# Sparse attention in three passes, an earlier second projection unit, forgetting values by channels, forgetting queries on 128 partitions, and narrower block levels in a two-model kernel

## The reference

```python
# sparse attention: 16 heads of 128 in 4 groups; 4 key blocks of 64 all chosen at this length
s = q @ k.T * scale; p = softmax(where(valid, s, NEG))
o = g0 * (p_c @ v_cmp) + g1 * (p_s @ v_sel) + g2 * (p_w @ v_win)
y = (silu(gate) * o) @ w_out

# mixer of the second model (w_in gives gq, gk, gv, gz, gb, ga, fq, fk, fv, ff)
a_mat = where(strict, (k @ k.T) * decay * beta, 0)         # gated delta heads, 4 of 128
u, w = triangular_solve(a_mat + eye, [v * beta, k * beta * exp(gc)])
s = fq @ fk.T * 64**-0.5 + (c_i - c_j); o_fox = softmax(causal(s)) @ fv   # 8 heads of 64
h = h + concat(o_gdn, o_fox) @ w_out
h = h + swiglu(rmsnorm(h)); return rmsnorm(h)[16:]
```

## Time and profile before

| | |
|---|---|
| median of 3 runs | 990.27 us (990.2 to 990.33) |
| profiled execution: its time | 988.4 us |
| its span | 986.6 us |
| granted TensorE clock, mean | 0.998 |
| PE busy | 968.6 us, 98% |
| PE weight loads | 853.3 us, 86% |
| DVE busy | 621.9 us, 63% |
| ACT busy | 472.1 us, 48% |
| POOL busy | 116.4 us, 12% |

### The profile page before, as it was taken

The page is one execution under the profiler, slowest core; times in us unless marked ns, Lnnn a source line. Parts: engine busy times, 40 slices in busy tenths (PEclk is TensorE's granted clock), DMA queues, the critical chain, the costliest instruction groups (busy, mean ns, idle before and its releaser), DMA issues.

```text
span 986.6 us, 15771 instructions
## 1 busy us (share of the span) xinstructions
PE 968.6 (98%) x6364; PEld 853.3 (86%) x6364; DVE 621.9 (63%) x887; ACT 472.1 (48%) x816; POOL 116.4 (12%) x117
## 2 busy tenths in 40 slices
PE   8999999999999999999999999999999999999996
PEld 7988778778998999998778789987888899999885
DVE  4964457556884655666654477986655666766533
ACT  6234446446545543455544456664435454444432
POOL 1000022010410000101320003212320101111000
PEclk9999999999999999999999999999999999999999
DMA  8745445445556753332015454522001355555551
GB/s 310 265 155 173 164 136 174 170 168 187 186 181 213 261 209 129 126 131 87 1 38 177 170 180 151 176 93 86 8 37 44 129 192 191 194 194 191 196 188 43
DMA packets 23372, 150.55 MB, mean 153 GB/s; under 512 B 3548, under 2 KB 3832, under 8 KB 5896
## 3 DMA queue, kind: packets, MB, share of 16 engines
q1 hardware_dynamic: 22960, 149.39, 43.4%
q10 hardware_dynamic: 344, 0.18, 0.1%
HBM read 148.50 MB, written 1.05 MB: 152 GB/s over the span
## 4 chain that ended last, share of the span: by engine, by line
PE 95%; DVE 2%; DMA 1%; ACT 1%; issue 0%; POOL 0%; POOLq 0%; SPq 0%; DVEq 0%; ACTq 0%
PE psum L689 91%; PE psum L768 1%; PE psum L1083 1%; DMA ring<-in_weights 1%; PE psum L1390 0%; DMA h<-in_x 0%; DVE ring_parts L1901 0%; ACT R L1509 0%; PE psum L1089 0%; PE psum L1251 0%; PE psum L1212 0%; PE psum L1255 0%; DVE xT_parts L529 0%; DVE xn L2437 0%; ACT L520 0%
## 5 line engine op out<-in xcount | busy, mean ns | idle before, releaser
L1901 DVE TENSOR_TENSOR ring_parts<-ring,high_parts 128x1024 fp32r<-128x1024 f32 (+1 forms) x272 | 334.0, 1266 | 161.1 <-ACT high_parts L1502 160.2
L1502 ACT CAST high_parts<-ring 128x1024 fp32r<-128x1024 f32 x268 | 268.0, 1049 | 204.9 <-PE psum L689 164.0
L689 PE MATMUL psum<-xT_parts,high_parts 128*128 128x256 f32 (+1 forms) x960 | 216.9, 285 | 2.8 <-DVE ring_parts L1901 2.3
L689 PE MATMUL psum<-xT_parts,ring_parts 128*128 128x256 f32 (+1 forms) x672 | 192.4, 286 | 0.0
L689 PE MATMUL psum<-high_parts,R_parts 128*128 128x512 f32 (+1 forms) x592 | 177.5, 375 | 1.1 <-DVE R_parts L529 1.1
L689 PE MATMUL psum<-high_parts,xT_parts 128*128 128x512 f32 (+1 forms) x528 | 171.0, 400 | 0.0
L689 PEld LDWEIGHTS psum<-xT_parts,high_parts 128*128 128x128 f32 x960 | 162.8, 189 | 4.4 <-DVE ring_parts L1901 2.9
L689 PE MATMUL psum<-R_parts,high_parts 128*128 128x256 f32 x832 | 156.5, 277 | 0.0
L689 PEld LDWEIGHTS psum<-R_parts,high_parts 128*128 128x128 f32 x832 | 130.3, 188 | 0.0
L689 PEld LDWEIGHTS psum<-xT_parts,ring_parts 128*128 128x128 f32 x672 | 126.7, 189 | 0.1
L689 PEld LDWEIGHTS psum<-high_parts,R_parts 128*128 128x128 f32 (+1 forms) x592 | 105.0, 179 | 21.8 <-issue 1.3
(11 more groups left out here) (306 smaller groups left out, 1085.0 us busy)
## 6 DMA issues: line engine op xcount, KB each, us to landing
ring<-in_weights SPq DMA_DIRECT2D x136, 1024.0 KB, 4.9
h<-in_x SPq DMA_DIRECT2D x4, 256.0 KB, 4.4
ring<-in_weights SPq DMA_DIRECT2D x4, 256.0 KB, 5.7
G<-in_gains SPq DMA_DIRECT2D x2, 512.0 KB, 7.3
out<-xn SPq DMA_DIRECT2D x2, 512.0 KB, 3.1
R<-in_ret_tabs SPq DMA_DIRECT2D x1, 768.0 KB, 11.4
tab<-in_tabs SPq DMA_DIRECT2D x1, 663.5 KB, 6.0
G<-in_p_t SPq DMA_DIRECT2D x1, 512.0 KB, 6.9
```

The costliest lines, as they stand in the source:

```text
L689: return pe.matmul(out, lhsT, rhs, start=first, stop=last, skip_group_check=True)
L1502: act.copy(as_r(hi), value).then_inc(sem("units_high"), 1)
L1901: return dve.tensor_tensor(as_r(value), value, value_of(hi), ALU.subtract)
```

## The change

- Start: unit 1 is loaded in halves, unit 3 ahead of the retention tables, and split_up_to(3) stands where split_up_to(2) did; ACT makes a small copy before its first real work, and PE a matmul without use among the turns.
- ret_w_out's units are ordered by row half first, then by column half; yT 1 is turned behind row half 0 of column half 0.
- Sparse attention's P·V becomes three one-pass products: V is split once into four high and four low parts, the turned probabilities of each step by ACT (high) and DVE (low). nsa_order puts step i+1's T ahead of step i's O.
- Forgetting queries: each head has its own 128x256 area with zeros in the other head's 64 rows, cleared by POOL; the meta columns are left out; DVE writes two halves. fox_scores then uses all 128 partitions.
- Forgetting values are made by channels (fv, 4 tiles, from A units) and turned on PE (vT) behind level 1's z; the order around Q is changed with it.
- Levels: z and y are computed for the odd blocks' columns alone.
- End: the last unit's products go row block by row block, and row block 0 is normed and stored by itself, in halves on three engines.

```diff
-    b("ret_w_out", 0, D, 16)
+    units.extend(("ret_w_out", "B", k0 + 4 * i, c0) for k0 in (0, 8) for c0 in (0, 512) for i in range(2))
...
-    b("w_in_2", 3080, 512)
+    a("w_in_2", 3080, 512)
...
+    order = [("S", 0), ("S", 1), ("N", 0), ("N", 1), ("C", 0), ("G", 0), ("T", 0), ("G", 1), ("S", 2), ("N", 2)]
+    last = len(STEPS) - 1
+    for i in range(last):
+        order += [("T", i + 1)] + [("G", i + 2)] * (i < 2)
+        if i + 3 <= last:
+            order.append(("S", i + 3))
+        order.append(("O", i))
+        if i + 3 <= last:
+            order.append(("N", i + 3))
+    return order + [("O", last)]
...
-             ("fin", 7), ("A", 2), ("A", 0), ("fv", 0, 0)] + [("Lz", 0, c) for c in level_chunks(0)]
-    order += [("fv", 0, 1), ("Q", 1), ("fv", 0, 2), ("Qm", 1), ("Q", 2), ("fv", 1, 0), ("Qm", 2), ("kv", 1), ("fv", 1, 1),
-              ("kv", 2), ("fv", 1, 2), ("Fs", 0), ("kv", 0)]
-    beside = {1: ([("Fn", 0), ("Fs", 1)], [("Ft", 0)]), 2: ([("Fn", 1), ("Fs", 2)], [("Fo", 0), ("Ft", 1)]),
+             ("fin", 7), ("A", 2), ("A", 0), ("fv", 0)] + [("Lz", 0, c) for c in level_chunks(0)]
+    order += [("Q", 1), ("fv", 1), ("Qm", 1), ("Q", 2), ("fv", 2), ("Qm", 2), ("kv", 1), ("fv", 3), ("kv", 2), ("Fs", 0),
+              ("kv", 0)]
+    beside = {1: ([("Fn", 0), ("vT", 1), ("Fs", 1)], [("vT", 2), ("vT", 0), ("Ft", 0)]), 2: ([("Fn", 1), ("Fs", 2)], [("Fo", 0), ("Ft", 1)]),
...
+        def fox_query(hd):
+            return nw[:, hd * T:(hd + 1) * T] if hd < 4 else R[:, R3 + (hd - 4) * T:R3 + (hd - 3) * T]
...
+        def odd_blocks(ap, lv):
+            return ap.rearrange("p (b two m) -> p b two m", two=2, m=LEVELS[lv])[:, :, 1, :]
...
-            for u in (1, 2):
-                unit(u, weights[u])
+            half = UNIT // 2
+            load("second_half", ring[:, UNIT:UNIT + half], weights[1, :, 0:half])
+            sp.dma_start(ring[:, UNIT + half:2 * UNIT], weights[1, :, half:UNIT]).then_inc(sem("unit_in1"), 16)
+            unit(2, weights[2])
+            unit(3, weights[3])
             load("ret_in", R[:, R4:R4 + NRT], ret_tabs)
-            unit(3, weights[3])
...
+                if f == 1:
+                    mm(psum[:, 3, 0:T], xn[:, 0:P], xn[:, 0:T], True, True)
...
-                        v0 = R2 + br * 1024 + k * 512 + g * P
-                        ins = mm(o.rearrange("p (n q) -> p n q", n=nh), R[:, v0:v0 + P], p_t[:, k], False,
-                                 br == 1 and k == kt - 1)
+                        v = [part[:, g * P:(g + 1) * P] for part in nsa_value_parts(2 * br + k)]
+                        p_t = [part[:, :, k * T // kt:(k + 1) * T // kt] for part in turned_p(i, br)]
+                        ins = parts3(mm, o.rearrange("p (f t) -> p f t", f=2), v, p_t, False, br == 1 and k == kt - 1)
...
-                    q0 = R3 + c0 + M + b * P
-                    mm(o, R[p0:p0 + FD, q0:q0 + P], R[p0:p0 + FD, R3 + 4 * TM + c0:R3 + 4 * TM + c0 + n], True, False)
+                    mm(o, fox_query(hd)[:, b * P:(b + 1) * P], R[:, R3 + 4 * TM + c0:R3 + 4 * TM + c0 + n], True, False)
...
+                first = M if name == "fin" and j < 4 else 0
                 for k in range(KD):
-                    ins = parts3(product, bank[:, 0:TM], w(k, slice(j % 2 * P, (j % 2 + 1) * P)), x_src(k, 0, TM),
+                    ins = parts3(product, bank[:, first:TM], w(k, slice(j % 2 * P, (j % 2 + 1) * P)),
+                                 x_src(k, first, TM - first), k == 0, k == KD - 1)
...
+            def value_rows(c):
+                t0, m = CHUNKS[c]
+                wait_read(pe, main, ("fv", 3))
+                bank = aux.open(pe, ("vT", c))
+                for j in range(4):
+                    ins = pe.transpose(bank[0:m, j * P:(j + 1) * P], value_cols(j, c), ident)
+                aux.full(ins, ("vT", c))
...
-                        ins = mm(bank[0:n, hd * n:(hd + 1) * n], of_head(level_rows(lv, c), c, hd), mat(PTb, C_ALL, c, hd),
-                                 True, True)
+                        ins = mm(bank[0:n, hd * n // 2:(hd + 1) * n // 2].rearrange("p (b m) -> p b m", m=LEVELS[lv]),
+                                 of_head(level_rows(lv, c), c, hd), odd_blocks(mat(PTb, C_ALL, c, hd), lv), True, True)
...
-            for c in range(2):
-                for t in range(TT):
+            for t in range(TT):
+                for c in range(2):
                     for k in range(2):
                         ins = parts3(product, banks[c, t], hidden_src(20 + k, t), w(k, slice(c * 512, (c + 1) * 512)),
...
+            act.wait_ge(sem("eps_set"), 1)
+            act.copy(cst[:, 9:10], eps1)
...
-                    bank = wait(aux, ("wT", i))
-                    c0 = i % 2 * 1024 + 512
-                    aux.free(act.copy(PTb[:, c0:c0 + 512], bank), ("wT", i))
+                    for br, name in enumerate(("sT", "wT")):
+                        bank = wait(aux, (name, i)).rearrange("p (f t) -> p f t", f=2)
+                        act.copy(as_r(turned_p(i, br)[0]), bank).then_inc(sem("turned_p"), 1)
...
-            split_up_to(2)
+            split_up_to(3)
...
+                        dve.wait_ge(sem("turned_p"), 2 * i + br + 1)
+                        hi, lo = turned_p(i, br)
+                        aux.free(dve.tensor_tensor(as_r(lo), bank, value_of(hi), ALU.subtract), (name, i))
...
+                    if j < 4:
+                        dve.wait_ge(sem("query_zeros"), 2)
+                        for half in range(2):
+                            rows_ = slice(half * FD, (half + 1) * FD)
+                            ins = dve.scalar_tensor_tensor(fox_query(2 * j + half)[rows_, :], bank[rows_, M:TM],
+                                                           float(FD) ** -0.5, token_scale[rows_, M:TM], ALU.mult, ALU.mult)
...
+                if jj == 4:
+                    pool.memset(nw[:, :], 0.0).then_inc(sem("query_zeros"), 1)
+                if jj == 7:
+                    pool.memset(R[:, R3:R3 + 4 * T], 0.0).then_inc(sem("query_zeros"), 1)
...
-            norm(7)
+            for t in range(TT):
+                total = last_sums(t)
+                pool.wait_ge(sem("last_sums"), 2 * t + 1)
+                own.then_wait(pool.tensor_scalar(total[:, 2:3], total[:, 0:1], EPS, None, ALU.add))
+                pool.wait_ge(sem("last_sums"), 2 * t + 2)
+                root = rstd[:, 14 + t:15 + t]
+                own.then_wait(pool.tensor_tensor(root, total[:, 1:2], total[:, 2:3], ALU.add))
+                pool.tensor_tensor(root, root, power, ALU.pow).then_inc(sem("last_root"), 1)
```

More of the change, by code:

```diff
@@ L231, in main_uses @@
     u += [(("fin", j), "dve") for j in range(8)]
-    u += [(("fv", c), "act") for c in range(3)]
+    u += [(("fv", j), "dve") for j in range(4)]
     u += [(("gz", t), "act") for t in range(TT)]
@@ L236, in main_uses @@
         u += [(("fg", n), "dve"), (("fu", n), "dve")]
-    u += [(("dn", c, t), "dve") for c in range(2) for t in range(TT)]
+    u += [(("dn", c, t), "dve") for t in range(TT) for c in range(2)]
     return u
@@ L289, in splits_beside @@
 def splits_beside(kind, key):
-    return kind in ("fin", "gz") or kind == "fv" and key[1] < 2 or kind == "mo" and key != [1, 1]
+    return kind in ("fin", "fv", "gz") or kind == "mo" and key != [1, 1]
 def mixer_uses():
@@ L918, in _, with retention_output @@
                         turn_half("yT", 0, R3)
[L920 to L927 removed]
+            def retention_output(k0, c):
+                for kk in (k0, k0 + 4):
+                    w, product = next_unit(4)
+                    for t in range(TT):
+                        bank = main.at(("ro", c, t)) if kk else main.open(pe, ("ro", c, t))
+                        for k in range(4):
+                            ins = parts3(product, bank, out_src(kk + k, *rows0[t]), w(k, slice(0, 512)), kk + k == 0,
+                                         kk + k == 15)
+                        if kk == 12:
+                            main.full(ins, ("ro", c, t))
+            for k0 in (0, 8):
+                for c in range(2):
+                    if (k0, c) == (0, 1):
+                        pe.wait_ge(sem("ret_y"), 8)
+                        turn_half("yT", 1, R3)
+                    retention_output(k0, c)
             def ple(n, added, ready):
@@ L1759, in _ @@
                     split_up_to(item + HIGH - 1, 1)
-                if kind == "fv" and key[0]:
-                    c = key[1]
+                if kind == "vT":
+                    c = key[0]
                     m = CHUNKS[c][1]
-                    bank = main.wait(act, ("fv", c))
+                    bank = aux.wait(act, ("vT", c))
                     c0 = R3 + 8 * TM + c * 512
-                    main.free(act.activation(R[0:m, c0:c0 + 512], bank[0:m, :], ACT.Copy,
-                                             scale=rstd[:, 9 + c:10 + c] if c else 1.0), ("fv", c))
+                    aux.free(act.activation(R[0:m, c0:c0 + 512], bank[0:m, :], ACT.Copy,
```

(10 more changed lines are left out.)

152 lines of the change are left out of this document (103 added, 49 removed).

## The result

The changed kernel takes 974.03 us (median of 4 runs, 973.14 to 975.99) against 990.3 in the same job (4 runs, 990.2 to 990.39): ratio 0.9843, 95% interval 0.9832 to 0.9855. The profiled execution took 973.14 us with a span of 971.6, 15.0 under the span before. The page: busy times, and the chain by engine.

A forecast was written before the change was run, and what follows sets the result against it. TensorE, busy 98% of the span, was taken to bound the kernel. Gains and losses summed to -11.05 us, so 977.4 us profiled and 979.2 as median, with a range of 972.5 to 985 for 8 in 10.

The forecast's parts named there:

- the case with the highest chance: The forecast as summed, 979.2 us as median, with its own range of 976 to 982; chance 0.55.
- Start: Kernel start: early table load -1.1 us, unit 3's load and split earlier -1.35; sum -2.45.
- P·V in three passes: Sparse attention: -0.33 us on each of 12 steps, -3.96 on PE, +0.2 for waits in the last two; sum -3.8.
- Forgetting queries at the projection: Four query tiles: -0.96 us on PE without meta columns, double writes +1.05, clears +1.9; net +2.0.
- the clears I price at 1.9: POOL clearing two 128x1024 areas at the projection would hold DVE's two-input operations: +1.9 us, bounds 0 and 4.2.
- Values by channels: Value projection: products from 16.7 to 12.1 us, plus 12 turns of two records, 2.65; sum -1.9.
- Q1: Behind level 0's z products, PE waits for a bank that DVE frees late: +1.5 us, bounds 0 and +3.
- Scores: Forgetting scores on 128 partitions: a head from 1.51 to 1.06 us, -3.9 in all, 0.8 lost to banks; -3.1.
- Levels: z and y records falling from 128 to 64 columns stay about 0.11 us apart: 0, bounds 0 and -11.5.
- Tail: Kernel end: -0.6 us on POOL, -0.6 on the scaling, about -1.0 on the store; sum -2.2.
- B: Rival, nothing blocks: clears free (-1.9), Q1 covered (-1.5), scores full (-0.8), giving 975.0 us; chance 0.12.
- D: Rival: sparse attention's step chain becomes the bound, subtractions held by POOL's multiply, +18 us, 997; chance 0.04.

The follow-up runs named there:

- no_table_copy: The changed kernel without ACT's small first copy, so its table load comes with its first real work: 976.97 us, ratio 0.9877.
- nsa_old_order: The changed kernel with sparse attention's phases in the old order, three passes kept: 983.41 us, ratio 0.993.
- fv_before_q: The changed kernel with one value projection put back between level 0 and Q1: 973.74 us, ratio 0.9834.
- split_first: The changed kernel with VectorE splitting the third key projection's unit ahead of the decay rows instead of behind them: 973.47 us, ratio 0.9836.
- fv_and_split: The changed kernel with one value projection ahead of Q1 and the third key projection's unit split ahead of the decay rows: 971.86 us, ratio 0.9821.
- warm_and_both: The fv_and_split kernel with four useless matmuls among the first turns instead of one: 971.32 us, ratio 0.9816.

## Why the prediction was right, and where it was off

The time lies in the range (972.5 to 985) and in the case with the highest chance, a gain that comes out of PE's stream; its size was put 5 us too low. Of the 3.95 us by which the profile is better than the sum, 1.93 lie in the mixer, and there two errors hid each other: the parts gave more than forecast, and a stretch of low clock took some 1.5 back. In no_table_copy, whose mixer is the same and has no such stretch, the stage is 7.0 us shorter than before, twice the forecast of 3.5. Step by step:

- **Start** (-2.45; -2.88 measured). Right as a whole, wrong inside: undone one at a time, the loads cost 2.7 and the table copy 0.7, together more than the whole. The mis-sized step is "unit 1 in halves keeps it from becoming late": true, but I had given it no price, and whole, the unit costs a wait of 0.62.
- **ret_w_out** (-1.1; -1.34, and 1.3 when undone). Right.
- **P·V in three passes** (-3.96 on PE, +0.2 in waits). The PE term is somewhat too large: by sums of start-to-start times, from the product with the compressed keys' values ahead of P·V to the end of P·V and without waits, the twelve steps fell from 28.1 to 24.7 us, -3.4. The wait term is too pessimistic: 1.38 became 0.94, not 1.6. With small differences elsewhere the stage gained 4.3. That the new order carries the gain is shown by nsa_old_order, and by more than the sum of durations had suggested.
- **Forgetting queries at the projection** (+2.0; +1.3). The double writes did cost, through DVE: PE's waits in that stage rose from 0.43 to 2.29 us. Each tile takes DVE 0.88 from start to start (635.92 to 636.80) against 0.35 before (648.04 to 648.39 in the earlier trace rows), so +0.53 and not +0.35. PE then waited for a unit's low part, which DVE made late, and not for a bank of fin as I had put it. The clears, priced at 1.9, cost nothing. The failed step is "the clears I price at 1.9"; "if POOL's clears leave DVE alone" was one of my own signs of being wrong, and it is what happened. What the Trainium skill's "SBUF — State Buffer", section "Who interferes with whom", says agrees here: beside the clear, which reads nothing, the two-input DVE operation kept its 0.43, while beside POOL's copies one took 2.77 instead of 1.21. That rule's figure for the part, +0.1, was nevertheless further off than mine, because the writes cost DVE 1.6 for the three tiles and not 1.05, and PE waited 1.54 for the split behind them.
- **Values by channels** (-1.9; -2.5). Sums of start-to-start times: 17.3 us became 13.4 for the products and 1.4 for the turns. The products ran partly at the low clock; without it they take 12.5 (no_table_copy), and the part gives 3.4. I had counted two records for a turn; the trace has one, at 0.11, which is 1.2 of the difference.
- **Q1** (+1.5; +1.23). Right in size. fv_before_q shows that cover takes the wait away; split_first, that the wait comes from POOL's level parts beside DVE's subtraction (1.98 us, and 0.99 where they come later), as I had read it in the kernel before.
- **Scores** (-3.9 on PE, 0.8 lost). PE's sum fell by 3.2 us (12.0 to 8.8), because a head still takes 1.1 to 1.15 and not 1.06, and nothing was lost to banks. The result, -3.1, was right by two errors.
- **Levels** (0; -0.9). Right in kind: 0.05 to 0.1 for each 16 products, under a tenth of what columns would give in all. The rule of the Trainium skill, "TensorE: Matmul & The Clock Gate", section "LDWEIGHTS (loading the stationary operand)", and the trace agree after as before: 0.111 to 0.114 us a record with 64 columns.
- **Tail** (-2.2; -2.3). Right as a whole; no run takes its parts asunder.

Of the rivals, B (nothing blocks) was partly true, in its clears. D, the slower case, did not come, and the subtractions kept their 0.69 while POOL's multiply of 1.90 ran; but nsa_old_order shows that the chain it named is real: without the new order the change would have given back more than half of all it gained.

Not foreseen was the clock. The changed kernel's times spread over 2.9 us in one job and 5.6 in the other, those of the kernel before over 0.2 in the first job and 1.8 to 2.6 in the others. The mean clock of the latter was 0.992 to 0.998, so it may well be low in places there too; of these no trace exists.

## What to carry to other kernels

Narrowing the moving side of a matmul from 128 columns to 64 bought next to nothing (0.9 us of 11.5) while the stationary side stayed 128 wide; widening K from 64 to 128 with zeros bought a quarter of the scores' time (12.0 to 8.8 us), with the zeros written once. When a pass is made cheaper by more preparation on other engines, move the use one step away from the preparation in the same change, or the preparation's chain becomes the bound. And place a split that TensorE waits for ahead of small, latency-bound operations on the same engine: here one line moved gave 1.7 us of the stage. Before the gains of two fixes are added up, look in the trace of the first whether the second wait is still there.

## What was not expected of the hardware

TensorE's granted clock fell to the lower level for some 3.5 us at a time, in one to three places of 11 of the 13 profiles of the changed kernel and its variants: in the mixer in ten of them (at 652 to 657, near 662 to 677, mostly 1 to 4 us behind Q1's start, and once at 748 to 752), behind the waits of 2.15 and 1.96 us in nsa_old_order, and in three profiles around the end of the wait for x. One such stretch cost 1.3 to 1.6 us. What decides whether it comes is open, and PE's waits alone don't: waits of 1.94 and 3.05 us for x went by without one, and so did both of the mixer's waits in no_table_copy, while split_first, which has neither of the two, has one in the mixer. fv_and_split and warm_and_both have neither wait and no low stretch there. A clear by POOL (0.95 us for 128x1024) did not hold a DVE operation with two SBUF inputs, copies by POOL did (2.77 us instead of 1.21).
